# Delta rule's inverse in 64-token blocks and sliding attention two heads at a time, in a kernel of one core

## The reference

```python
    s = jnp.einsum('bnqhgd,bnkhd->bnhgqk', qb, kb).astype(f32) * (DH ** -0.5)
    s = jnp.where(mask[None, :, None, None], s, -jnp.inf)
    sink = jnp.broadcast_to(sinks.astype(f32).reshape(1, 1, HKV, G, 1, 1), s.shape[:-1] + (1,))
    p = jax.nn.softmax(jnp.concatenate([s, sink], axis=-1), axis=-1)[..., :-1]
    o = jnp.einsum('bnhgqk,bnkhd->bnqhgd', p.astype(v.dtype), vb)
```

```python
    a_mat = jnp.einsum('bhnik,bhnjk->bhnij', k_beta, k) * decay_strict
    t_mat = lax.linalg.triangular_solve(a_mat + eye, jnp.broadcast_to(eye, a_mat.shape),
                                        left_side=True, lower=True, unit_diagonal=True)
    u = jnp.einsum('bhnij,bhnjv->bhniv', t_mat, v_beta)
    w = jnp.einsum('bhnij,bhnjk->bhnik', t_mat, k_beta * jnp.exp(g)[..., None])
    def step(S, inp):
        q_c, kt_c, u_c, w_c, qk_c, gl_c = inp
        v_new = u_c - jnp.einsum('bhck,bhkv->bhcv', w_c, S)
        o_c = jnp.einsum('bhck,bhkv->bhcv', q_c, S) + jnp.einsum('bhij,bhjv->bhiv', qk_c, v_new)
        S = S * jnp.exp(gl_c)[..., None, None] + jnp.einsum('bhck,bhcv->bhkv', kt_c, v_new)
        return S, o_c
```

## Time and profile before

| | |
|---|---|
| median of 3 runs | 2527.01 us |
| the profiled execution's own time | 2525.99 us |
| its span | 2524.2 us |
| PE busy over the span | 2437.4 us (97%) |
| DVE busy | 1432.2 us (57%) |
| ACT busy | 1065.5 us (42%) |
| rounds 0 to 6 of the mix | 163.50 to 209.74 us |
| rounds 7 to 22 (all level steps but the last) | 209.74 to 301.23 us |
| round 23 to the end of `w` (round 25) | 301.23 to 310.57 us |

### The profile page before, as it was taken

One profiled execution on the slowest core, in us unless ns is written; L12 is line 12 of the kernel. 1 busy time (PEld: TensorE's weight loads), 2 busy tenths in 40 slices (PEclk: granted clock), 3 DMA queues, 4 the chain that ended last, 5 costly groups with the idle time before them and its releaser, 6 DMA issues. The chain is left out here.

```text
span 2524.2 us, 31546 instructions
## 1 busy us (share of the span) xinstructions
PE 2437.4 (97%) x12854; PEld 2011.7 (80%) x12854; DVE 1432.2 (57%) x2177; ACT 1065.5 (42%) x1831; POOL 264.6 (10%) x248
## 2 busy tenths in 40 slices
PE   8999989999999799999999999999999999999997
PEld 6768878888887688888887787888887778888886
DVE  6537756443357765344375567745476454776355
ACT  5533236322336644232264464433253555544341
POOL 0021112000021530000032001100000000111000
PEclk9989999999999899999999999999999999999999
DMA  5210012222222213222221122222222112222221
GB/s 194 84 42 1 1 42 93 100 92 100 92 84 92 75 67 106 95 92 100 92 98 59 45 99 92 96 97 94 82 94 75 43 43 84 89 96 101 92 90 61
DMA packets 59248, 206.48 MB, mean 82 GB/s; under 512 B 6704, under 2 KB 8800, under 8 KB 58976
## 3 DMA queue, kind: packets, MB, share of 16 engines
q1 hardware_dynamic: 58464, 201.35, 22.8%
q0 software_dynamic: 640, 3.12, 0.3%
HBM read 202.30 MB, written 2.10 MB: 81 GB/s over the span
## 5 line engine op out<-in xcount | busy, mean ns | idle before, releaser
L264 PE MATMUL ps<-XH,WH 128*128 128x512 f32 (+1 forms) x2216 | 832.6, 376 | 46.4 <-DVE XL L1976 13.5
L265 PE MATMUL ps<-XL,WH 128*128 128x512 f32 (+1 forms) x2216 | 812.1, 366 | 0.0
L266 PE MATMUL ps<-XH,WL 128*128 128x512 f32 (+1 forms) x2216 | 812.0, 366 | 0.0
L237 DVE TENSOR_TENSOR WL<-RAW,WH 128x1024 fp32r<-128x1024 f32 (+1 forms) x382 | 465.2, 1221 | 244.5 <-ACT WH L229 243.5
L264 PEld LDWEIGHTS ps<-XH,WH 128*128 128x128 f32 x2216 | 420.7, 190 | 132.7 <-issue 35.2
L265 PEld LDWEIGHTS ps<-XL,WH 128*128 128x128 f32 x2216 | 420.7, 190 | 69.9 <-issue 5.3
L266 PEld LDWEIGHTS ps<-XH,WL 128*128 128x128 f32 x2216 | 420.1, 190 | 68.2
L229 ACT ACTIVATE WH<-RAW 128x1024 fp32r<-128x1024 f32 (+1 forms) x382 | 391.3, 1036 | 164.1 <-DMA RAW<-in_w 127.5
L264 PE MATMUL ps<-H,WH 128*128 128x512 f32 (+1 forms) x1104 | 407.1, 369 | 2.0 <-ACT AR L1879 2.0
L265 PE MATMUL ps<-H,WH 128*128 128x512 f32 (+1 forms) x1104 | 405.7, 368 | 0.0
L266 PE MATMUL ps<-H,WL 128*128 128x512 f32 (+1 forms) x1104 | 405.6, 367 | 0.0
(11 more groups left out here) (375 smaller groups left out, 2468.8 us busy)
## 6 DMA issues: line engine op xcount, KB each, us to landing
RAW<-in_w SPq DMA_DIRECT2D x128, 512.0 KB, 3.2
RAW<-in_up SPq DMA_DIRECT2D x88, 512.0 KB, 3.2
RAW<-in_dn SPq DMA_DIRECT2D x32, 512.0 KB, 3.2
RAW<-in_hyb SPq DMA_DIRECT2D x23, 512.0 KB, 3.3
RAW<-in_qkv SPq DMA_DIRECT2D x18, 512.0 KB, 3.2
RAW<-in_kvf SPq DMA_DIRECT2D x17, 512.0 KB, 3.3
RAW<-in_rin SPq DMA_DIRECT2D x16, 512.0 KB, 3.2
RAW<-in_dn SPq DMA_DIRECT2D x16, 384.0 KB, 3.0
```

The costliest lines, as they stand in the source:

```text
L237: dve.e.tensor_tensor(WL[:, s, 0:n], RAW[:, s, 0:n], f32(WH[:, s, 0:n]), ALU.subtract).then_inc(*w_lo.at(u))
L264: pe.e.matmul(out, wh, xh, start=first, stop=False)
L265: pe.e.matmul(out, wh, xl, start=False, stop=False)
L266: return pe.e.matmul(out, wl, xh, start=False, stop=last)
```

## The change

The inverse is built for the two diagonal blocks of 64 rows of each chunk separately, in levels 1 to 5, and level 6 joins them. The product of a step becomes 8 products of 64x64x64 (`halves`): for each of 4 chunks the block in rows 0 to 63 and that in rows 64 to 127, written to the same half of the same bank. DVE's operations of levels 1 to 5 have 256 columns where they had 512. Level 6 has two steps of 4 products of 64x64x64. Level 0 moves from POOL to DVE (two operations of 64 rows and one of 128), POOL clears the full matrix, ACT copies the diagonal blocks into it after level 5 (`fd`), and DVE writes the joined block into it. The transpose `tf` becomes 8 products with the identity.

The attention takes the two heads of a key pair together: 16 jobs instead of 32, one slot in every round, between heads 1 and 2. The order in a slot is values, transposes, masking products, scores. The maxima and sums of two heads lie in adjacent columns, and the small DVE operations take both at once. The scaling by the inverse sum moves from DVE to ACT. The table of level masks shrinks.

```diff
-C0 = [("cos", 512), ("sin", 512), ("mi", 128), ("ms", 128), ("lv", 896), ("sel", 512), ("slide", 256)]
+C0 = [("cos", 512), ("sin", 512), ("mi", 128), ("ms", 128), ("lv", 384), ("idc", 64), ("sel", 512), ("slide", 256)]
...
-        window = Attention("win", window_jobs, (4, 5), (6,))
...
+            def scores(s):
+                j, n = WIN[s]
+                k0, nk = win_keys(s)
+                for hp in range(2):
+                    if s:
+                        pe.wait_ge(at_x, (s - 1, hp))
+                    else:
+                        claim(pe, 4 + hp)
+                    pe.e.matmul(PS[4 + hp][:, 0:nk], identb, slide[:, 256 - nk:256], start=True, stop=False)
+                for hp in range(2):
+                    lo = 64 * hp
+                    pe.e.matmul(PS[4 + hp][:, 0:nk], QA[j][lo:lo + 64, 128 * n:128 * n + 128], KA[lo:lo + 64, 128 * k0:128 * n + 128],
+                                start=False, stop=True).then_inc(*at_s.at((s, hp)))
...
+                for hp in range(2):
+                    pe.wait_ge(at_n, (s, hp))
+                    for x in range(win_keys(s)[1] // 128):
+                        at = 256 * hp + 128 * x
+                        mm = pe.e.transpose(PS[6][:, at:at + 128], win_p(s, hp)[:, 128 * x:128 * x + 128], ident)
+                mm.then_inc(*at_t.at(s))
...
+                for x in range(nk // 128):
+                    for hp in range(2):
+                        lo = 64 * hp
+                        mm = pe.e.matmul(PS[7][lo:lo + 64, 128 * n:128 * n + 128], VA[:, 128 * (k0 + x) + lo:128 * (k0 + x) + lo + 64],
+                                         win_pt(s, hp, x), start=x == 0, stop=x == nk // 128 - 1)
+                mm.then_inc(*at_o.at(s))
...
+            for i in range(len(WIN) + 3):
+                if 0 <= i - 3:
+                    out(i - 3)
+                if 0 <= i - 2 < len(WIN):
+                    turn(i - 2)
+                if i < len(WIN):
+                    scores(i)
+                yield
...
+                    for hp in range(2):
+                        dve.wait_ge(at_x, (s, hp))
+                    dve.e.tensor_tensor(win_cols(s, 2), win_cols(s, 2), win_cols(s, 3), ALU.add).then_inc(*at_r.at((s, "sum")))
+                    dve.wait_ge(at_r, (s, "sum"))
+                    dve.e.reciprocal(win_cols(s, 4), win_cols(s, 2)).then_inc(*at_r.at((s, "1/l")))
+                if i < len(WIN):
+                    j, n = WIN[i]
+                    sinks = vec("sink", j, 5)[:, 0:5:4]
+                    for hp in range(2):
+                        dve.wait_ge(at_s, (i, hp))
+                        mx = dve.e.reduce_max(win_cols(i, 0)[:, hp:hp + 1], PS[4 + hp][:, 0:win_keys(i)[1]], AXX, negate=True)
+                    mx.then_inc(*at_mx.at(i))
+                    dve.wait_ge(at_mx, i)
+                    dve.e.scalar_tensor_tensor(win_cols(i, 1), sinks, -1.0, win_cols(i, 0), ALU.mult, ALU.min).then_inc(*at_m.at(i))
+                    dve.wait_ge(at_m, i)
+                    dve.e.tensor_tensor(win_cols(i, 3), sinks, win_cols(i, 1), ALU.add).then_inc(*at_m.at((i, "sinks")))
...
+                    act.wait_ge(at_r, (s, "1/l"))
+                    for hp in range(2):
+                        act.e.activation(win_p(s, hp), win_p(s, hp), ACT.Copy, scale=win_cols(s, 4)[:, hp:hp + 1]).then_inc(*at_n.at((s, hp)))
...
+                    act.e.activation(win_cols(i, 3), win_cols(i, 3), ACT.Exp)
+                    for hp in range(2):
+                        act.e.activation(win_p(i, hp), PS[4 + hp][:, 0:win_keys(i)[1]], ACT.Exp, bias=win_cols(i, 1)[:, hp:hp + 1],
+                                         accum_out=win_cols(i, 2)[:, hp:hp + 1]).then_inc(*at_x.at((i, hp)))
...
+            def halves(key, a, b):
+
+                for c in range(4):
+                    for lo in (0, 64):
+                        mm = pe.e.matmul(P[lo:lo + 64, 64 * c:64 * c + 64], a(c, lo), b(c, lo), start=True, stop=True)
+                mm.then_inc(*did.at(key))
...
-            turn("tf", f_)
-            yield
-            for lv in range(1, 7):
+            halves("tf", block(e_, 1), lambda c, lo: ident[lo:lo + 64, lo:lo + 64])
+            yield
+            for lv in range(1, 6):
                 if lv == 1:
                     pe.wait_ge(act, "Tt0")
                 else:
                     pe.wait_ge(dve, ("T", lv - 1))
-                four(("y", lv), c_, e_)
+                halves(("y", lv), decays, block(e_))
                 yield
                 pe.wait_ge(dve, ("y", lv))
-                if lv < 6:
-                    four(("t", lv), f_, a_)
-                    yield
-                    pe.wait_ge(dve, ("Tt", lv))
-                four(("s", lv), a_, f_)
-                if lv < 6:
-                    yield
+                halves(("t", lv), block(e_, 1), block(a_))
+                yield
+                pe.wait_ge(dve, ("Tt", lv))
+                halves(("s", lv), block(a_), block(e_, 1))
...
+            pe.wait_ge(dve, ("T", 5))
+            for c in range(4):
+                mm = pe.e.matmul(P[64:128, 64 * c:64 * c + 64], c_[0:64, 128 * c + 64:128 * c + 128], block(e_)(c, 0), start=True, stop=True)
+            mm.then_inc(*did.at(("y", 6)))
+            yield
+            pe.wait_ge(dve, ("y", 6))
+            for c in range(4):
+                mm = pe.e.matmul(P[0:64, 64 * c:64 * c + 64], block(a_)(c, 64), block(e_, 1)(c, 64), start=True, stop=True)
+            mm.then_inc(*did.at(("s", 6)))
             yield
             pe.wait_ge(pool, "ka")
+            pe.wait_ge(act, "fd")
...
+            act.wait_ge(dve, ("T", 5))
+            act.wait_ge(pool, "zero")
+            for lo in (0, 64):
+                fd = act.e.activation(by4(f_[lo:lo + 64, :])[:, :, lo:lo + 64], by64(blocks(e_, 1)[lo:lo + 64, :]), ACT.Copy)
+            fd.then_inc(*did.at("fd"))
...
-            dve.wait_ge(pool, "mo")
-            dve.e.tensor_tensor(by4(f_), each(ident), by4(e_), ALU.subtract).then_inc(*did.at("T0"))
-            yield
-            yield
-            for lv in range(1, 7):
+            dve.wait_ge(did, "at")
+            for lo in (0, 64):
+                mo = dve.e.tensor_tensor(by64(blocks(a_, 1)[lo:lo + 64, :]), by4(c_[lo:lo + 64, :])[:, :, lo:lo + 64],
+                                         level(0)[lo:lo + 64], ALU.mult)
+            mo.then_inc(*did.at("pairs"))
+            dve.wait_ge(did, "pairs")
+            dve.e.tensor_tensor(by64(blocks(e_, 1)), c0("idc")[:, None, :].broadcast_to([128, 4, 64]), by64(blocks(a_, 1)),
+                                ALU.subtract).then_inc(*did.at("T0"))
...
-                dve.e.tensor_tensor(by4(a_), by4(P), each(c0("lv")[:, 128 * lv:128 * lv + 128]), ALU.mult).then_inc(*did.at(("y", lv)))
+                dve.e.tensor_tensor(by64(blocks(a_)), by64(P[:, 0:256]), level(lv), ALU.mult).then_inc(*did.at(("y", lv)))
...
+            dve.wait_ge(pe, ("y", 6))
+            dve.e.tensor_copy(a_[64:128, 0:256], P[64:128, 0:256]).then_inc(*did.at(("y", 6)))
+            yield
+            dve.wait_ge(pe, ("s", 6))
+            dve.wait_ge(pool, "zero")
+            dve.e.tensor_scalar(by4(f_[0:64, :])[:, :, 64:128], by64(P[0:64, 0:256]), -1.0, None, ALU.mult).then_inc(*did.at(("T", 6)))
...
-            pool.wait_ge(dve, "at")
-            pool.e.tensor_tensor(by4(e_), by4(c_), each(c0("lv")[:, 0:128]), ALU.mult).then_inc(*did.at("mo"))
+            pool.e.memset(f_, 0.0).then_inc(*did.at("zero"))
...
-                for g in heads[0:2] + ([att] if rounds % 2 else []) + heads[2:4] + [att]:
+                for g in heads[0:2] + [att] + heads[2:4]:
...
```

More of the change, by code:

```diff
@@ L1511, in build_program, with win_keys, win_p, win_pt @@
-        window = Attention("win", window_jobs, (4, 5), (6,))
+        WIN = [(j, n) for j in range(4) for n in range(4)]
+        def win_keys(s):
+            _, n = WIN[s]
+            return max(n - 1, 0), 128 * (n + 1 - max(n - 1, 0))
+        def win_p(s, hp):
+            return TM[:, s % 3, 256 * hp:256 * hp + win_keys(s)[1]]
+        def win_pt(s, hp, x):
+            return TM[:, 3 + s % 2, 256 * hp + 128 * x:256 * hp + 128 * x + 128]
+        def win_cols(s, k):
+            at = 10 * (s % 3) + 2 * k
+            return COL[:, at:at + 2]
@@ new lines, in window_pe, with turn, out @@
+        def window_pe(pe):
+            def scores(s):
[11 more added lines that the diff above has]
+                                start=False, stop=True).then_inc(*at_s.at((s, hp)))
+            def turn(s):
+                if s:
+                    pe.wait_ge(at_e, s - 1)
+                else:
+                    claim(pe, 6)
+                for hp in range(2):
[4 more added lines that the diff above has]
+                mm.then_inc(*at_t.at(s))
+            def out(s):
+                j, n = WIN[s]
+                k0, nk = win_keys(s)
+                if n == 0:
+                    if j:
+                        pe.wait_ge(x_lo, ("hwo", j - 1))
```

(23 more changed lines are left out.)

200 lines of the change are left out of this document (57 added, 143 removed).

## The result

The changed kernel takes 2486.5 us (median of its four runs), against 2526.5 of the kernel before measured beside it: a ratio of 0.9837, 95% interval [0.9823, 0.9850], 40 us less. Forecast were 2495 us, in a range from 2482 to 2520.

A forecast was written before the change was run, and what follows sets the result against it. PE was taken as the bound, busy for 97% of the span. Rounds 7 to 22 give -32.2 us, the preparing rounds -1, round 23 to `w` +1: -32.2 in all, median 2495 us, 8-in-10 range 2482 to 2520.

The forecast's parts named there:

- The level steps: Rounds 7 to 22: 64 steps fall from 0.895 to 0.60 us each, 57.3 to 38.4 us in all.
- the ends: Bounds for one level step: 0.45 us if pairs run at once, 1.16 us if products run one after another.
- L2581's 0.055 us a record: Rate read from 128-column products overlapping in one bank; at it, a level step's sixteen records would take 0.88 us.
- second rival: Level steps: pairs writing one bank do not overlap; step taken as 1.0 us, kernel 2520 us; chance 0.20.
- The attention: Rounds 7 to 22: scores, masks, transposes, values and changes of shape of the two-head slots take 20.9 us on PE.
- Both fit: Attention rounds of 4.55 us: DVE's 3.3 us and ACT's 3.1 us of work both fit in.
- Rounds 0 and 1: Preparing rounds at half clock: two fewer score slots save some 3 us.
- Rounds 2 to 6: Preparing rounds: fewer slots give -1 us on PE, DVE's level 0 masking +2, `tf` as products 4 x 0.15.
- Round 23 to `w`: Behind the levels: POOL's chain stays, PE has less to do while waiting; +1 us for the clock, from 0 to +4.
- 1 (no overlap): Level steps: pairs do not overlap, a step is 0.88 to 1.16 us, taken as 1.0; kernel 2520 us; chance 0.20.
- 2 (the attention's chain paces the rounds): Attention rounds: scores wait for the previous slot's exponentials; 12 rounds give 11 us, kernel 2506 us; chance 0.12.
- 3 and 4 (the clock): Half clock late, rounds 19 to 25: 2505 us, chance 0.10; or through all levels: slower, 2554 us, chance 0.08.

The follow-up runs named there:

- The attention alone: Only the attention's half of the change (slots of two heads), inverse as in the kernel before: 2507.7 us, ratio 0.9917 to the kernel before; traced once more at 2505.6 us.
- inverse alone: Only the inverse in blocks of 64, attention one head at a time as in the kernel before: 2509.1 us, ratio 0.9923 to the kernel before.
- halves not in pairs: Changed kernel, with a level step's 8 products issued as four of one half, then four of the other: 2493.4 us, ratio 0.9859 to the kernel before.
- `ka` first: Changed kernel, but POOL makes `ka` of all four heads before the first `kl`: 2483.2 us, ratio 0.9824 to the kernel before.
- slot last: Changed kernel, but each round's attention slot comes behind heads 2 and 3 instead of between heads 1 and 2: 2490.4 us, ratio 0.9854 to the kernel before.

## Why the prediction was right, and where it was off

The time lay in the stated range and moved as forecast, by 40 us where 32 were forecast. Term by term:

**The level steps (-19 us forecast): mechanism right, size off.** Pairs on opposite quarters of the array run at once though both write one bank. The step took 0.467 us, not 0.60: 64 x 0.133 = 8.5 us more gain than taken. The choice between the ends was wrong: it leaned on L2581's 0.055 us a record as if that were a limit of PE's starting rate, while there it was half the streaming time of 128 columns. The same kernel has the comparison. In level 6 the four products of a head, and those of all four heads, use one tile; 16 products take 1.69 us. Read one by one, their records start 0.058 us apart, 0.117 a product, and three records at each end run beside the neighbouring step, which makes 0.106 a product on average. In the paired steps it is 0.058. The order of issue alone, in the experiment above, is worth 0.11 to 0.15 us a step.

The Trainium skill, TensorEngine Tiling (Array Packing), Gotcha 1 (PSUM Pressure), says that different row tiles cannot access the same PSUM bank at the same time. This trace does not agree for two tiles that also write different partitions of the bank: one after the other, 8 products at 0.117 us would be 0.94 us a step, and 0.467 were measured. (The prediction calls this case its second rival; it is the first in its list.)

```profile
259.19 0.27 PE L1615 MATMUL ps<-AR,XF 64*64 64x64 f32 x1
...
260.88 0.27 PE L1620 MATMUL ps<-AR,XF 64*64 64x64 f32 x1
```

**The attention (20.9 us in these rounds): right**, 21.0 measured by what is left over, 21.2 read slot by slot.

**What the sum lacked: the output bank, +5.2 us.** The step that failed is "Both fit": it added up what DVE and ACT have to do in a round of 4.55 us and found 3.3 and 3.1. (Its terms for ACT add up to 2.8, which changes nothing here.) It counted only what recurs in every slot; the hand-over of the outputs, once in four slots, was left out, and so was its place at the end of ACT's slot. Moving it gave back 4.9 us in the trace. The wait would have come at the forecast step of 0.60 us too, at an estimated 1.0 us where it was 1.58: PE came to the bank after 5.47 - 1.58 = 3.89 us, and 4 x 0.133 more are 4.42. The two errors of this stretch (8.5 us gain too little, 5.2 of waits left out) partly cancelled: -35.4 where -32.2 stood. That is luck: without these waits the kernel takes 2480.5 us, as measured, and 2482 was the lower end of the range.

**Rounds 0 and 1 (-3): -5.7, half of it unforeseen.** The term took away the two slots' own work, and that part was right: the slots take 2.9 us instead of 5.6. It overlooked that half as many slots make other products neighbours: the products with 4 contraction rows take 11.2 us instead of 14.5, and a wait of 0.4 is new. The attention alone shows the same 14.49 us, and with the slot moved the pairs vanish and these products take 14.1 again.

**Rounds 2 to 6: within 1.5 us.** The terms were -1 for the slots, +2 for DVE's mask of level 0, +0.6 for `tf`; +0.17 was measured. The parts alone give -1.7 and +5.9, so the sum holds only with both together. One wait for that mask is there (0.94 us, for L1723), as before there was one of 1.43.

**Round 23 to `w` (+1 for the clock): nothing.** PE waits there 0.70, 0.85 and 0.85 us for POOL, less idle than feared, and the clock stayed at 1.00. POOL's chain was 8.06 us busy, unchanged:

```profile
264.74 1.16 PE L1556 MATMUL ps<-AR,XF 128*128 128x128 f32 x8 [0.70 <-POOL XF L1795]
...
268.75 1.16 PE L1556 MATMUL ps<-Y,XF 128*128 128x128 f32 x8 [0.85 <-POOL XF L1795]
```

**The rivals.** 1 (no overlap): refuted by 0.467 us. 2 (the attention's chain paces the rounds): refuted for scores and exponentials, no PE wait for ACT in rounds 7 to 18; but its kin, the hand-over of the outputs, was there at half its price (5.2 of 11 us). 3 and 4 (the clock): refuted in the trace of the changed kernel, 1.00 in all of rounds 7 to 22. The granted clock did fall in other executions (inverse alone, halves not in pairs, `ka` first, slot last), each time right behind idle stretches of PE before round 8, for 3.5 to 7 us; the changed kernel had the same gaps (0.94 and 2.08 us) and no fall. What decides between the two stays open. The fall cost 1.5 us with `ka` first, 1.6 with the halves not in pairs, by their traces.

## What to carry to other kernels

When an engine's round gets 30% shorter, list for each bank or buffer when it is given back, also what happens once in several rounds: a copy at the end of a slot that nobody waited for becomes a wait, here as soon as a round is under 5.5 us. Independent small products should be put in turn on different rows and columns of the array, and work between two such groups can cost more than its own time, as the attention's slot did in rounds 0 and 1. A rate read where something else is the limit is no bound: 0.055 us a record was streaming, not issue. And two parts of a change tested alone need not add up: 34.7 us alone were 41.4 together.
